# A stage's last output tile, its norm row and the next stage's first three units made for half of the tokens at a time

## The reference

```python
for l in range(DEPTH):                       # DEPTH = 2
    h = swiglu_ffn(rms_norm(x, ffn1_norm_pre[l]), ffn1_w_in[l], ffn1_w_out[l])
    x = x + 0.5 * rms_norm(h, ffn1_norm_post[l])
    h = rms_norm(x, mix_norm_pre[l]) @ mix_w_in[l]
    o_gdn = gated_deltanet_group(h, ...)     # 4 heads of 128, chunks, a scan over them
    o_cm = conformer_conv_group(h, ...)      # 512 channels, 31 taps, layer norm
    h = jnp.concatenate([o_gdn, o_cm], axis=-1) @ mix_w_out[l]
    x = x + rms_norm(h, mix_norm_post[l])
    h = swiglu_ffn(rms_norm(x, ffn2_norm_pre[l]), ffn2_w_in[l], ffn2_w_out[l])
    x = x + 0.5 * rms_norm(h, ffn2_norm_post[l])
    x = rms_norm(x, block_norm[l])
```

## Time and profile before

| | |
|---|---|
| three runs | 2075.77, 2075.79, 2076.00 us; median 2075.79 us |
| profiled execution | 2076.07 us, its span 2074.3 us |
| mean granted TensorE clock | 0.993 |
| PE busy, PEld busy | 2037.9 us (98%), 1705.3 us (82%) |
| DVE busy, ACT busy, POOL busy | 1159.9 us (56%), 786.3 us (38%), 35.5 us (2%) |
| boundaries between two stages (start of the first unit) | 385.5, 665.4, 1032.4, 1405.2, 1685.1 us |

### The profile page before, as it was taken

The page is one execution under the profiler, slowest core; times in us unless marked ns, Lnnn a source line. Parts: engine busy times, 40 slices in busy tenths (PEclk is TensorE's granted clock), DMA queues, the critical chain, the costliest instruction groups (busy, mean ns, idle before and its releaser), DMA issues.

```text
span 2074.3 us, 25854 instructions
## 1 busy us (share of the span) xinstructions
PE 2037.9 (98%) x9832; PEld 1705.3 (82%) x9832; DVE 1159.9 (56%) x1617; ACT 786.3 (38%) x1192; POOL 35.5 (2%) x62
## 2 busy tenths in 40 slices
PE   7999999999999999999999999999999999999998
PEld 6888888877987888888878888888889888888886
DVE  5654522699875745532374554338998565555323
ACT  5222232458655422222242222225576643222223
POOL 1000000011000000000000000000100000000000
PEclk9999999999999999999999999999999999999998
DMA  5333333376112333333323333334740123333321
GB/s 158 104 99 101 91 99 95 82 163 139 25 52 71 102 101 93 92 98 94 89 81 102 100 92 94 93 105 101 161 108 21 56 73 114 93 91 98 94 82 41
DMA packets 350400, 194.29 MB, mean 94 GB/s; under 512 B 8851, under 2 KB 345205, under 8 KB 350325
## 3 DMA queue, kind: packets, MB, share of 16 engines
q1 hardware_dynamic: 344058, 176.34, 29.6%
q0 software_dynamic: 4608, 16.78, 4.4%
q10 hardware_dynamic: 1658, 0.16, 0.1%
HBM read 174.38 MB, written 2.10 MB: 85 GB/s over the span
## 4 chain that ended last, share of the span: by engine, by line
PE 85%; DVE 11%; ACT 1%; issue 1%; DMA 0%; SPq 0%; DVEq 0%; ACTq 0%
PE res L494 24%; PE res L496 23%; PE res L495 23%; DVE u L1685 4%; DVE cacc L1767 2%; PE stat L501 1%; PE res L566 1%; PE pq L800 1%; PE pq L791 1%; PE res L567 1%; PE res L570 1%; PE pq L494 1%; PE pq L496 1%; PE pq L495 1%; PE bc L528 1%
## 5 line engine op out<-in xcount | busy, mean ns | idle before, releaser
L1035 ACT ACTIVATE wh<-raw 128x1024 fp32r<-128x1024 f32 (+1 forms) x336 | 348.2, 1037 | 985.7 <-PE res L496 980.7
L494 PE MATMUL res<-xh,wh 128*128 128x512 f32 x1560 | 612.1, 392 | 5.6 <-DVE xl L1532 3.0
L495 PE MATMUL res<-xl,wh 128*128 128x512 f32 x1560 | 608.1, 390 | 0.0
L496 PE MATMUL res<-xh,wl 128*128 128x512 f32 x1560 | 608.0, 390 | 0.0
L1518 DVE TENSOR_TENSOR wl<-raw,wh 128x1024 fp32r<-128x1024 f32 (+1 forms) x304 | 363.1, 1195 | 381.7 <-ACT wh L1035 381.7
L494 PEld LDWEIGHTS res<-xh,wh 128*128 128x128 f32 x1560 | 293.6, 188 | 67.5 <-DVE Um L1896 3.1
L496 PEld LDWEIGHTS res<-xh,wl 128*128 128x128 f32 x1560 | 293.4, 188 | 61.7
L495 PEld LDWEIGHTS res<-xl,wh 128*128 128x128 f32 x1560 | 293.7, 188 | 60.2 <-issue 0.5
L494 PE MATMUL res<-hh,wh 128*128 128x512 f32 x704 | 273.9, 389 | 0.0
L495 PE MATMUL res<-hl,wh 128*128 128x512 f32 x704 | 273.9, 389 | 0.0
L496 PE MATMUL res<-hh,wl 128*128 128x512 f32 x704 | 273.9, 389 | 0.0
(11 more groups left out here) (309 smaller groups left out, 1973.8 us busy)
## 6 DMA issues: line engine op xcount, KB each, us to landing
raw<-in_ffn_w_in SPq DMA_DIRECT2D x176, 512.0 KB, 3.8
raw<-in_ffn_w_out SPq DMA_DIRECT2D x64, 448.0 KB, 3.6
raw<-in_mix_w_in SPq DMA_DIRECT2D x48, 512.0 KB, 4.0
raw<-in_ffn_w_out SPq DMA_DIRECT2D x32, 512.0 KB, 3.8
wl<-raw POOLq DMA_DIRECT2D x32, 512.0 KB, 5.3
raw<-in_mix_w_out SPq DMA_DIRECT2D x16, 512.0 KB, 3.9
xin<-in_x SPq DMA_DIRECT2D x4, 512.0 KB, 5.1
out_dram<-xin SPq DMA_DIRECT2D x4, 512.0 KB, 3.7
```

The source lines that it names most:

```text
L494: pe.matmul(bank, wh[:, slot, j, :], hi, start=first, stop=False)
L495: pe.matmul(bank, wh[:, slot, j, :], lo, start=False, stop=False)
L496: return pe.matmul(bank, wl[:, slot, j, :], hi, start=False, stop=last)
L1035: act.activation(wh[:, slot, 0:nk, :], raw[:, slot, 0:nk, :], ACT.Copy).then_inc(hi_full, 1)
```

## The change

At five of the six stage ends (not the last) the work is cut into tokens 0 to 255 (h = 0) and 256 to 511 (h = 1).

- The last output tile's products are made first for h = 0, into another bank, then for h = 1: 132 products of 256 columns in place of 66 of 512 (48 in place of 24 in the mixer). The weights of a unit are free (`unit_done`) only when h = 1 has used them.
- Squares, sums, root, reciprocal, spread, updates, `xh` and `xl` are made for each half; sums and spread of h = 0 lie between the products of h = 1, those of h = 1 between the first products of the next stage.
- The first three units are multiplied for all k of h = 0, then for all k of h = 1: 144 products of 256 columns in place of 72 of 512.
- `idle_products` stay only at the last stage end.
- After an FFN the units 1 and 2 of the next stage are made into `wh` and `wl` between the updates, no longer before them.
- Mixer: four taps a layer leave the table `taps`, `SCAN_TAPS` takes them, and the spread for the convolution's norm moves ahead by five tiles (15 products). The spread's wait for `udiag` moves with it.
- The loop over m in the FFN's output is written out on PE.

```diff
@@ PE
+            def half_sums(stage, l, h):
+                if h == 0:
+                    pe.wait_ge(half_sq, 3 * l + stage + 1)
+                else:
+                    pe.wait_ge(ysq_ready, l * 3 * KD + (stage + 1) * KD)
+                for c in HALF_C[h]:
+                    mm = pe.matmul(stat[:, c:c + 1], sqr[:, (KD - 1) % 2, c * P:(c + 1) * P], ones[:, 0:1],
+                                   start=False, stop=True, skip_group_check=True)
+                mm.then_inc(ssq_full if h else half_ssq, 1)
...
-                for k in range(KD if stage or l else 0):
-
-                    pe.wait_ge(xh_ready, l * NXS + stage * KD + k + 1)
...
+                for h in range(2 if stage or l else 0):
+                    t = HALF[h]
+                    for k in range(KD):
...
+                            if k == 0 and h == 0:
+                                pe.wait_ge(lo_full, l * UNITS + (u0 + n + 1 + SLOTS))
+                            pe.matmul(banks[n][:, t], wh[:, n, k, :], xh[:, k, t], start=k == 0, stop=False)
+                            pe.matmul(banks[n][:, t], wl[:, n, k, :], xh[:, k, t], start=False, stop=False)
...
+                        if (h, k) == (0, 0) and before != 1:
+                            half_sums(before, bl, 1)
+                        if (h, k) == (0, 2):
+                            half_spread(before, bl, 1)
...
+                                mm = tile(to[:, t], n % SLOTS, j, hh[:, k, t], hl[:, k, t], k == 0, k == KF - 1)
+                                if m == KD - 1 and halved(stage, l):
+                                    if (h, part, j) == (0, 1, 6):
+                                        first_sums(stage, l)
+                                    if (h, part, j) == (1, 0, 2):
+                                        half_sums(stage, l, 0)
+                                    if (h, part, j) == (1, 1, 1):
+                                        half_spread(stage, l, 0)
...
+                        if (k, m) == (CT - 1, 0):
+                            pe.wait_ge(udiag, l + 1)
+                            spread_column(rcol).then_inc(uvbc_full, 1)
...
-                    if k == 1:
-                        pe.wait_ge(udiag, l + 1)
-                        spread_column(rcol).then_inc(uvbc_full, 1)
...
+                            if (h, half, k) == (0, 1, 2):
+                                first_sums(1, l)
+                            if (h, half, k) == (1, 0, 3):
+                                half_sums(1, l, 0)
+                    mm.then_inc(unit_done if h else half_done, 1)
+                half_spread(1, l, 0)
+                half_sums(1, l, 1)
@@ ACT
+                        y_half(0, gain, stage, q, l)
+                        for k in range(4):
+                            if k % 2 == 0:
+                                high(u0 + IN_U + 3 * KD + 1 + k // 2, 1 + k // 2, 8, l)
+                            input_half(k, 0, ns, gn, nl)
@@ DVE
+                    half_column(0, before, bl)
+                    dve.wait_ge(half_bc, 3 * bl + before + 1)
+                    for h in range(2):
+                        if h:
+                            dve.wait_ge(bc_full, rows_before(bl, 2 * before + 1) + 1)
+                        for k in range(KD + 1):
+                            if k < KD:
+                                update_half(k, h, before, bl)
+                            if k >= 1:
+                                low_half(k - 1, h, stage, gain, l, before, bl)
+                            if h == 0 and k in (1, 3) and stage != 2:
+
+                                weight_low(u0 + (k + 1) // 2, (k + 1) // 2, 8, l)
+                            if h == 0 and k == 4:
+                                half_column(1, before, bl)
...
-                        (1, 1, 0), (1, 1, 3), (1, 1, 1)]
+                        (1, 1, 0), (1, 1, 1), (1, 0, 0)]
...
-                SCAN_TAPS = ((8, 2, 1), (7, 2, 0), (CT * CTAPS, 0, 0), (0, 0, 0))
+                SCAN_TAPS = ((9, 2, 1), (7, 2, 1), (3, CT * CTAPS, 0), (0, 0, 0))
```

More of the change, by code:

```diff
@@ L337, in pre_gain, with halved, last_bank, spread_bank @@
             return gpre[:, l, :] if l else call[:, 0, G_F1PRE:G_F1PRE + KD]
+        HALF = (slice(0, T // 2), slice(T // 2, T))
+        HALF_C = (range(0, NC // 2), range(NC // 2, NC))
+        def halved(stage, l):
+            return not (stage == 2 and l == L - 1)
+        def last_bank(h, bank):
+            return in_bank(4) if h == 0 else bank
+        def spread_bank(h):
+            return bc if h == 0 else in_bank(5)
         ffn_w = [(ffn1_w_in, ffn1_w_out), (ffn2_w_in, ffn2_w_out)]
@@ L559, in first_units @@
                         mm.then_inc(unit_done, 1)
-                for k in range(KD if stage or l else 0):
-                    pe.wait_ge(xh_ready, l * NXS + stage * KD + k + 1)
[L563 to L572, removed]
+                before, bl = (stage - 1, l) if stage else (2, l - 1)
@@ L628, in ffn @@
                 pair(KF - 1, 1, KF - 2)
[L630 to L635, removed]
+                for m in range(KD):
+                    q = m % 4
+                    if m == 0:
+                        pe.wait_ge(h_ready, l * NP + (f * KF + KF - 1))
+                    pe.wait_ge(y_done, l * NY + (YB + stage * KD + m - 3))
+                    bank = in_bank(y_bank(q, stage, l))
+                    for h in range(2 if m == KD - 1 and halved(stage, l) else 1):
+                        t, to = slice(0, T), bank
+                        if m == KD - 1 and halved(stage, l):
+                            t, to = HALF[h], last_bank(h, bank)
@@ L649, in _ @@
+                            if t.stop == T:
+                                mm.then_inc(unit_done, 1)
+                            elif part == len(OUT_PARTS) - 1:
+                                mm.then_inc(half_done, 1)
+                if not halved(stage, l):
+                    y_sums(stage, l)
+                    spread([1, 5][f], l)
             for l in range(L):
@@ L993, in _ @@
                         weights(MIX_IN_U + m, l)
[L994 to L997, removed]
+                        if m < KD - 1:
+                            mix_out(m, 0)
+                    if m < KD - 1:
+                        mix_out(m, 1).then_inc(unit_done, 1)
+                for h in range(2):
+                    for half in range(2):
+                        hi, lo = (hic, loc) if half else (hig, log)
+                        for k in range(CT):
+                            mm = tile(last_bank(h, res[:, (KD - 1) % 4, :])[:, HALF[h]], (KD - 1) % SLOTS, half * CT + k, hi[:, k, HALF[h]],
+                                      lo[:, k, HALF[h]], half == 0 and k == 0, half == 1 and k == CT - 1)
+                            if (h, half, k) == (0, 1, 2):
[5 more added lines that the diff above has]
+                half_sums(1, l, 1)
                 ffn(1, l)
@@ L1049, in root, with input_half @@
                 act.activation(rsq[:], stat[:, 0:NC], ACT.Sqrt, bias=eps[:, 0:1], scale=1.0 / D).then_inc(root_ready, 1)
-            def inputs(stage, gain, u0, l):
-                for k in range(KD):
+            def input_half(k, h, stage, gain, l):
+                before, bl = (stage - 1, l) if stage else (2, l - 1)
+                if h == 0:
+                    act.wait_ge(half_x, (3 * bl + before) * KD + k + 1)
+                else:
+                    act.wait_ge(x_ready, l * NXR + ((stage - 1) * KD + k + 1))
+                act.activation(xh[:, k, HALF[h]], xt[:, k, HALF[h]], ACT.Copy,
+                               scale=gain[:, k:k + 1]).then_inc(xh_ready if h else half_xh, 1)
+            def inputs(stage, gain, u0, l):
+                if stage or l:
+                    for k in range(4, KD):
+                        input_half(k, 0, stage, gain, l)
+                    high(u0 + 3, 3, 8, l)
+                    for k in range(KD):
+                        input_half(k, 1, stage, gain, l)
+                for k in range(0 if stage or l else KD):
                     if stage == 0 and l == 0:
@@ L1648, in ffn @@
                     y_sum(m, 2 * f, l)
-                row([1, 5][f], l, rcol)
+                if not halved(2 * f, l):
+                    row([1, 5][f], l, rcol)
             for l in range(L):
```

136 lines of the change are left out of this document (109 added, 27 removed).

## The result

The changed kernel takes 2078.68 us (median of 18 runs, 2077.07 to 2082.34), the kernel before 2075.78 us (18 runs beside them, 2074.85 to 2077.22). The ratio is 1.0016, 95% interval 1.0009 to 1.0023: slower by 2.9 us, less than the 0.2% taken for "no change", but outside what chance explains, and on the other side of the -0.5 us that the prediction gave.

A forecast was written before the change was run, and what follows sets the result against it. It took chains at five stage boundaries, gaps of 5.9 us without products, as what can be won. Terms summed to +1.0 (120 ns) or -3.0 (113); -0.5 was taken: 2075.3 us on the median's scale, range 2070.5 to 2080.5.

The forecast's parts named there:

- no change: Whole kernel: the terms as summed, 2072 to 2079.5 us, changes under 0.2% (4.2 us) counting as none; chance 62%.
- The boundary as laid out: FFN boundary, three: last tile to unit 3 takes 37.8 us at 120 ns, 37.3 before; PE waits 1.9 to 2.2 us.
- Behind the mixer: Boundary behind the mixer, two: only 24 products cover the chain; +2.2 to +2.4 us each.
- 3 x 0.9: Three FFN boundaries at +0.9 us each, if a half product takes 120 ns.
- Inside the mixer: Two mixers: earlier spread -2.8 us a layer, plus the moved taps; layer 0 -4.8, layer 1 -2.5.
- The taps: Mixer, `turn_u(0)`: -2.6 us in layer 0, at most 0.3 won in layer 1; +0.6 charged in the scan.
- The fall that goes: Mixer of layer 1, behind the projection's wait: the clock's fall should go with the shorter wait, -1.6 us.
- The half product: PE product of 256 columns: 113 to 120 ns; 1212 halves for 606 products alone cost 0 to +8 us.
- rule on weight loads: PE: loads overlap matmuls only where row groups differ; some 0.1 us more per half, +120 us; trace goes against it.
- The clock behind the new waits: FFN boundaries: three new waits of 2 us may each bring a clock fall; half of 3 x 1.6 = +2.4 us.

The follow-up runs named there:

- the clock is held: Changed kernel with the keys' column sums split and eight idle products ahead of the wait for unit 2's weights at each FFN end: 2074.34 us.
- the kernel before with the sums split: Kernel before with only the column sums of the keys' squares split in two, a unit's 24 products between them: 2077.36 us, ratio 1.0008.
- the one with the sums split: Changed kernel with the column sums of the keys' squares split in two: 2078.2 us.
- the mixer part alone: Kernel before with only four taps a layer moved into the scan and the spread five tiles earlier: 2068.1 us, ratio 0.996.

## Why the prediction was right and wrong

**The boundary as laid out: right.** DVE was to start at t = 13.3 and started at 13.5 (378.37 - 364.89), the second `wl` was to be ready at 20.0 and was at 20.2, PE was to reach its wait at 18.1 for 1.9 to 2.2 us and waited 2.02. Unit 3 was to start at 37.8 and starts at 38.0 where the clock is held. Behind the mixer the waits were forecast at 0.7, 1.2, 0.9, 0.5 and 0.6 us and are 0.56, 1.11, 0.64, 0.19 and 0.39; end and stretch behind it cost 2.4 us for 2.2 to 2.4 forecast. With the clock held the three FFN ends cost 2.1 us and the stretch behind the second 0.6, 2.7 in all, which is 3 x 0.9.

**Inside the mixer: right in sum, by luck in layer 1.** It gave 4.2 us in each layer, 8.4 in all, against 7.3 and 1.6 for the fall, 8.9. In layer 1 two errors cancel. The taps were to cost 0.3 us there (0.3 won, 0.6 charged in the scan) and are worth 1.9. The fall that goes was to give 1.6 and gives nothing: in the kernel before, the mixer took 251.89 us in layer 1, with its falls, and 251.93 in layer 0, without them, and with the sums split 251.89 in layer 1 without any. What layer 1 loses to the clock it waits less: 0.21 us for 3.42 at `turn_u(0)`, and none of the three waits for `loc` (0.24, 0.41 and 0.39 us) that follow the one of 1.78 in layer 0. In the kernel before with the sums split, where that mixer has no fall, the taps win 1.9 us there.

**The half product: mis-sized by choice.** The two bounds were 113 and 120 ns, and the prediction took a value between them (-0.5 of -3.0 and +1.0). It is 120 (382.48 to 382.60). So 13 to 14 ns come on top of the columns at 256 and at 512 alike, and 606 more products cost 8 us. That alone is 1.5 of the 3.4 us by which the prediction missed. The Trainium skill's rule on weight loads (TensorE: Matmul & The Clock Gate, Part 3, The mechanism), weighed there at +120 us, is not borne out: 1212 halves go by at 120 ns, each with its load of 128 columns.

**The clock behind the new waits: the step that failed.** The prediction charged half of 3 x 1.6 = 2.4 us for them. In the profiled execution two of the three waits brought a fall and they cost 3.1 + 1.5 = 4.6 us. How many fall was put about right (two for one and a half); the size was not: a fall was priced at 1.6 us wherever it came, and at the first boundary it lasted longer (0.51 and 0.80 in two windows) and cost 3.1. The charge was 2.2 us short in the profiled executions; by the medians 1.9 us of the miss are left for it. By the medians too, idle products in the waits win back 2.5 us on the changed kernel and 3.9 on the one with the sums split.

At 120 ns the sum now closes on the 4.0 us between the two profiled executions: +2.7 for the FFN ends, +4.9 for the mixer's ends, -8.4 in the mixers, +4.6 for the falls and +0.2 ahead of the first end. The prediction had +2.7, +4.8, -8.9 and +2.4.

What stays open is where the clock falls. Waits of 2.01 us stand in front of both kinds of boundary in one execution (clock 1.00 behind the second FFN end, 0.74 behind the third), and edits far away move the falls. That the falls cost what they cost is shown by the pairs and by the stretches; no run shows a rule by which one could tell their places in advance.

## What to carry to other kernels

Halving a step to fill a gap is paid in every product that is halved: here 13 ns for each of 606 more products, 8 us, against a gap of which 3.3 us a boundary could be won and 2 us came back as a wait for the next operand. Before cutting, lay out the chain to the second and third operand, not the first. A wait of 2 us that takes the place of a gap filled with idle products is best filled as well, or the time it saves can be lost to the clock behind it. Compare kernels stretch by stretch and with the clock beside each: a fall can cost 3.1 us or nothing, by whether a later wait takes it up. And look at the long runs of small products: breaking up the one of 32 sums gave 3.3 us once the long waits were gone. The two small moves inside the mixer with that split are the version to keep, 10.8 us under the kernel before.

## What the runs showed that was not expected

- 32 column sums in one piece (3.6 us, PE busy throughout by its records) bring a fall of the clock in or just behind them in 13 of 18 places (two layers in the profiles of nine kernels, the five being layer 0 of the kernel before, and both layers with the mixer ends alone halved and with no idle products); in two pieces of 1.84 us with 24 products between them, in none of 16. A busy PE is not always one that keeps its clock.
- The gain of an edit depends on falls elsewhere: the same split wins 3.3 us on one kernel and nothing on another.
- A wide scatter between executions can come from the clock: the kernels with 5 to 7 us of it have their slow executions at a lower mean clock (0.991 against 0.994 with the mixer part alone). The reverse doesn't hold: the kernel before has three falls in its profile and a scatter of 2.4 us.
